# One product of the projection behind the turn of the combined probabilities, and the combination ahead of the product's read-out

## What is computed

```
q, k, v, z = h @ w_in            # 4 parts, 8 heads, v dim 256, two q/k maps of 128
sc   = q_m @ k_m.T * scale       # per head, map m = 0, 1; a chunk sees itself and earlier ones
attn = softmax(sc_0) - lam * softmax(sc_1)
o    = rms_norm(attn @ v) * subln * (1 - lambda_init) * silu(z)
out  = x + gate * rms_norm(o @ w_out)
```

## Time and profile before

| | us |
|---|---|
| median of 3 runs | 2139.18 |
| lowest, highest | 2137.22, 2139.21 |
| profiled execution, its own time | 2142.87 |
| its span | 2141.1 |
| TensorE busy in the span | 2001.4 (93%) |
| VectorE, ScalarE, GpSimd busy | 1276.9, 783.8, 578.6 |
| the seven passes of the loop, from about 861 to 1712 in the span | 851 |
| TensorE busy in these 851 | 819.2 |

### The profile page before, as it was taken

How to read it: one execution, slowest core, us unless ns; L and a number is a source line. 1 busy time by engine, 2 the same in 40 slices (tenths; PEclk the granted TensorE clock), 3 DMA queues, 4 the chain that set the end, 5 groups by cost and what they waited for, 6 DMA issues and landing times.

```text
span 2141.1 us, 26819 instructions
## 1 busy us (share of the span) xinstructions
PE 2001.4 (93%) x9444; PEld 1659.1 (77%) x9444; DVE 1276.9 (60%) x1996; ACT 783.8 (37%) x1563; POOL 578.6 (27%) x640
## 2 busy tenths in 40 slices
PE   3679999999999989899999999999999979999998
PEld 3668888888888868687787878788787868888886
DVE  3567666666566336577676767677676735434343
ACT  3233333333454323344343434444343424322241
POOL 1143333333456223232232323233142201000000
PEclk9989999999999999999999999999999989999999
DMA  8647666663556586576757676676766576466652
GB/s 266 215 136 246 215 198 219 199 190 128 181 179 229 195 311 216 173 225 197 215 184 226 196 208 210 194 220 190 228 189 199 184 258 198 126 189 199 200 158 79
DMA packets 390465, 426.53 MB, mean 199 GB/s; under 512 B 20054, under 2 KB 286396, under 8 KB 387772
## 3 DMA queue, kind: packets, MB, share of 16 engines
q1 hardware_dynamic: 390048, 424.76, 63.0%
q10 hardware_dynamic: 284, 0.05, 0.0%
HBM read 294.70 MB, written 130.03 MB: 198 GB/s over the span
## 4 chain that ended last, share of the span: by engine, by line
PE 85%; DVE 4%; DMA 4%; issue 3%; POOL 1%; SPq 1%; ACT 1%; DVEq 0%; POOLq 0%; ACTq 0%
PE ps L1522 27%; PE ps L1524 26%; PE ps L1523 26%; DMA q_dr<-ev 2%; PE ps L1627 1%; PE ps L1635 1%; DMA ada<-in_ada_w_dram 1%; PE ps L1605 1%; DVE acc L1111 1%; SPq L448 1%; POOL stg L713 1%; POOL sums L693 1%; DMA h_dr<-stg 1%; DVE blk L1138 1%; PE ps L1654 1%
## 5 line engine op out<-in xcount | busy, mean ns | idle before, releaser
L1522 PE MATMUL ps<-blk,ring 128*128 128x512 f32 x1536 | 612.2, 399 | 15.1 <-issue 7.6
L1524 PE MATMUL ps<-blk,ring 128*128 128x512 f32 x1536 | 600.7, 391 | 0.0
L1523 PE MATMUL ps<-blk,ring 128*128 128x512 f32 x1536 | 600.1, 391 | 0.0
L1522 PEld LDWEIGHTS ps<-blk,ring 128*128 128x128 f32 x1536 | 289.5, 188 | 75.7 <-issue 14.3
L1524 PEld LDWEIGHTS ps<-blk,ring 128*128 128x128 f32 x1536 | 289.3, 188 | 62.2
L1523 PEld LDWEIGHTS ps<-blk,ring 128*128 128x128 f32 x1536 | 289.9, 189 | 56.9
L1076 DVE TENSOR_TENSOR ring<-sums,ring 128x512 fp32r<-128x512 f32 x256 | 224.2, 876 | 130.5 <-ACT ring L796 128.4
L693 POOL TENSOR_TENSOR sums<-raw 128x512 f32<-128x512 f32 x128 | 192.6, 1505 | 316.4 <-DVE ring L1076 295.6
L796 ACT ACTIVATE ring<-sums 128x512 fp32r<-128x512 f32 x256 | 160.1, 626 | 192.8 <-PE ps L1524 187.4
L1076 DVE TENSOR_TENSOR ring<-raw,ring 128x512 fp32r<-128x512 f32 x192 | 161.7, 843 | 83.6 <-ACT ring L796 82.8
L693 POOL TENSOR_TENSOR sums<-sums,raw 128x512 f32<-128x512 f32 x128 | 186.0, 1453 | 26.1 <-DVE ring L1076 19.6
(11 more groups left out here) (156 smaller groups left out, 3158.3 us busy)
## 6 DMA issues: line engine op xcount, KB each, us to landing
raw<-in_diff_w_in_dram SPq DMA_DIRECT2D x64, 1024.0 KB, 7.0
ada<-in_ada_w_dram SPq DMA_DIRECT2D x128, 256.0 KB
d_dr<-cc SPq DMA_DIRECT2D x128, 256.0 KB, 2.7
cc<-d_dr SPq DMA_DIRECT2D x128, 256.0 KB, 3.7
w_raw<-in_diff_w_out_dram SPq DMA_DIRECT2D x128, 256.0 KB, 3.6
ada<-in_ada_w_dram SPq DMA_DIRECT2D x32, 512.0 KB
v_dr<-ev SPq DMA_DIRECT2D x64, 256.0 KB
q_dr<-ev SPq DMA_DIRECT2D x32, 512.0 KB
```

Of the source, the lines that this page charges most:

```text
L1522: MM(dst, a_hi, b_hi, start=start, stop=False, skip_group_check=True)
L1523: MM(dst, a_hi, b_lo, start=False, stop=False, skip_group_check=True)
L1524: return MM(dst, a_lo, b_hi, start=False, stop=stop, skip_group_check=True)
```

## The change

The list `SPREAD` goes from two (blocks 0 to 3) and three (blocks 4 to 7) products ahead of the turn to one and two, and from one behind it to two. The number of products in a block stays three and four. On VectorE the combination now stands ahead of the `take` of the last product before the turn in every block. In blocks 4 to 7 that is where it was (second slot); in blocks 0 to 3 it stood behind the `take` of the first slot.

```diff
-    SPREAD = [(2, 1)] * 4 + [(3, 1)] * 4
+    SPREAD = [(1, 2)] * 4 + [(2, 2)] * 4
...
                         weights(n)
                         if i == 0 and a:
                             out_scale(*before(a))
-                        if i == 1 and qb >= HT:
+                        if i + 1 == n0:
                             combine(h - 1, qb)
                         take(n)
-                        if i == 0 and qb < HT:
-                            combine(h - 1, qb)
                         posts(n)
```

## The result

| | us | runs |
|---|---|---|
| before, median (lowest, highest) | 2137.95 (2134.76, 2144.57) | 11 |
| changed kernel, median (lowest, highest) | 2149.42 (2145.86, 2153.07) | 11 |
| ratio, with its 95% interval | 1.0053 (1.0041 to 1.0065) | |
| span of the profiled execution, before and after | 2141.1, 2144.1 | |

The changed kernel is 11.5 us slower, 0.5%. The prediction said 2140.6, in a range of 2133.5 to 2149.0: 0.4 us above its upper end.

A forecast was written before the change was run, and what follows sets the result against it. TensorE, busy 93% of the span, was taken to bound the kernel. Costs 23.7 less gains 9.0, 6.9 and 6.4 gave +1.4 us; on the median's 2139.2 that made 2140.6 us, range 2133.5 to 2149.0.

The forecast's parts named there:

- Costs in blocks 4 to 7: Turn of the probabilities, one product less ahead, waits for the combination: 0.53, 1.07, 0.58 and 0.49 us a pass.
- Gain in block 4: Weighted sum no longer waits for the low half of the turned probabilities, `post_high` now standing behind `aT_high`: 9.0 us.
- Gain in block 2: Combination ahead of the `take` is hidden under product 6, so the v turn waits 0.98 us less a pass: 6.9 us.
- the clock: TensorE's clock no longer falls in block 2 after the shortened v turn wait: 4 x 1.6 = 6.4 us, bounds 0 and 6.4.
- Cost in block 3: Turn stalls 0.78 us a pass for the combination; bounds 0.1, or 0.78 + 1.28 if a further add holds up `prob`.
- blocks 0 to 2: Shorter rows to combine; combinations end 0.1 us (block 0) or more ahead of the free turn: no cost.
- the first rival: Blocks 1 and 3: GpSimd's next add begins before `prob`, which waits; 9 us, 15 with block 1; 2149.6 to 2156; chance 0.11.
- the forecast's 23.7: Sum of the turn's stalls in blocks 3 to 7: 3.45 us a pass, 24.2 in seven, less 0.5 in pass 7.

The follow-up runs named there:

- chained_early: chained_adds with the combination ahead of the first read-out in blocks 4 to 7 too, the new list in all blocks; 2121.06 us, ratio 0.9922 to before.
- mix4_early: Kernel before with the combination ahead of the first read-out in all blocks and the new split (2, 2) in block 4 alone; 2116.24 us.
- chained_adds: Changed kernel with each GpSimd weight add of a group but its first also waiting for the add before it; 2138.77 us, ratio 1.0000 to before.

## Why the prediction missed, step by step

The prediction had +1.4 us for the seven passes. In the first pair of profiles they are 10.9 us longer. By blocks, from masking matmul to masking matmul, all passes together (block 7 measured in passes 1 to 6; the measured column adds up to 10.9 before rounding):

| block | forecast, us | measured, us |
|---|---|---|
| 0 | 0 | +0.1 |
| 1 | 0 | +3.9 |
| 2 | -13.3 | -13.3 |
| 3 | +5.5 | +12.2 |
| 4 | -5.3 | -6.3 |
| 5 | +7.5 | +7.6 |
| 6 | +4.1 | +3.7 |
| 7 | +2.9 | +2.9 |

- **Costs in blocks 4 to 7** (0.53, 1.07, 0.58, 0.49 us a pass): right in each block, by the rows above and by chained_early.
- **Gain in block 4** (9.0 us): right in mechanism, since the wait is gone; block 4 gained 1.0 us more than the sum had. A wait too short to be recorded is part of it: pass 5 shows none in the kernel before, and its block 4 is still 0.3 us longer than in mix4_early, where TensorE waits for nothing there (16.8 against 16.5).
- **Gain in block 2** (6.9 us) and **the clock** (6.4 us): right for this pair of profiles. For the medians the clock's term is 4.8, so 6.4 was 1.6 too much.
- **Cost in block 3** (0.78 us a pass) and **blocks 0 to 2** ("No cost"): here is the fault. The step reads: "As in block 5 I let it end with the add, at 1032.64, and `prob` follows after 0.04 and takes 0.75". The coefficient did so; `prob` did not. It waited for GpSimd's next add and took 1.72 us. Block 3 cost 1.69 + 0.06 = 1.75 us a pass, and block 1 cost 0.53 + 0.06 = 0.59. That is 0.97 + 0.59 = 1.56 us a pass more than forecast, 10.9 us in all.

With this and the clock's 4.8 the sum is 1.4 + 10.9 + 1.6 = 13.9 us for the medians, against 11.5 measured. With the clock as profiled it is 12.3 against 10.9 in the passes, of which 1.0 is block 4. The rest of the gap between the medians, 1.4 us, is open; the interval of the ratio reaches from 8.8 to 13.9 us, so it can be chance.

The mechanism was on record as the first rival, with 0.11 of the chances, at 9 us from block 3 and 15 with block 1 (measured: 6.8 and 10.9, since `prob` was held up by 1.0 us and not by 1.28). That the time, 2149.42, stands next to the rival's 2149.6 is in part luck: block 1 took part, and both blocks cost less than the rival had. The rival was set aside for a gap of 0.14 us between two adds, taken from the earlier trace rows. That gap belongs to a pair in which the second add needs the first. For the pair of blocks 1 and 3 the trace of before had the answer, in pass 2, block 1:

```profile
1000.27 1.29 POOL L693 TENSOR_TENSOR sums<-sums,raw 128x512 f32<-128x512 f32 x1
1001.52 1.29 POOL L693 TENSOR_TENSOR sums<-raw 128x512 f32<-128x512 f32 x1
1002.77 1.29 POOL L693 TENSOR_TENSOR sums<-sums,raw 128x512 f32<-128x512 f32 x1
```

From start to start they take 1.25 us, less than the 1.29 of the record: there is no gap for `prob` to slip into. Block 3 itself shows it too. The add of the earlier trace rows ends at 1032.62, and the next one starts at 1032.59:

```profile
1032.59 1.28 POOL L693 TENSOR_TENSOR sums<-raw 128x512 f32<-128x512 f32 x1
```

Both ends of the cost were written down (0.78 and 0.78 + 1.28), and the value was taken from the wrong pair.

## What to carry to other kernels

When an instruction is moved onto a stretch in which two engines share something, look up in the trace the very pair of instructions that it will fall between. A gap between two dependent instructions says nothing about two independent ones; here 0.1 us of order decided over 1 us of wait, in two blocks of each of seven passes. And cover has two ends: the product taken from ahead of the turn gained 9 to 10 us in one block of eight, and its waits cost 24 us over all blocks with the adds in step (the forecast's 23.7, borne out by chained_adds) and about 35 without, so such a list is best set block by block, by which of the two waits ends last there.

## What the hardware did that was not expected

- An instruction of VectorE with two operands in SBUF (`prob`, 0.75 us) that starts 0.09 us behind a GpSimd add takes 1.72 us; if it starts 0.08 us ahead, it takes 0.75 and the add 1.81 instead of 1.25. An extra semaphore wait on GpSimd between independent adds, which delays each by some 0.15 us, made the kernel 10.65 us faster.
- TensorE's clock fell behind a wait of 1.85 us in 3 of 7 passes and behind one of 2.46 us in 6 of 14, but in none of 49 passes with waits of 0.93 and 1.48 us around one product, and not behind a single one of 2.31 us.
